# Second dense block: who copies out of PSUM, when the memory branch is gated, and in which order TensorE takes its products

## The reference

```python
h = rms_norm_2(x, g_mix);  proj = h @ w_in
u_ssm, q, k, v, qi, ki, wi, qm, gates = jnp.split(proj, offs, axis=-1)
y_ssm = s5_branch(u_ssm, ...)    # b_bar @ u, a complex linear scan over 256 tokens, real(c @ states),
                                 # + d_skip * u, gelu, then y * sigmoid(y @ w_glu)
y_dsa = dsa_branch(q, k, v, ...) # 8 heads of 64, keys chosen by an index score (a mask), softmax
y_mem = memory_branch(qm, km, vm)# 4 heads of 128 over 256 memory rows, softmax
g_s, g_d, g_m = jnp.split(jax.nn.sigmoid(gates), N_BRANCHES, axis=-1)
merged = g_s * (y_ssm @ w_up_ssm) + g_d * (y_dsa @ w_up_dsa) + g_m * (y_mem @ w_up_mem)
x = x + merged @ w_out
x = x + hier_moe(rms_norm_2(x, g_ffn), ...)   # 32 experts, all of w_gate, w_up, w_down read
```

## Time and profile before

| | us |
|---|---|
| median of 3 runs | 2243.97 |
| the profiled execution | 2246.94 |
| its span, first to last instruction | 2245.1 |
| TensorE busy | 1842.2 (82%) |
| VectorE busy | 812.1 (36%) |
| ScalarE busy | 497.7 (22%) |
| mean rate from memory over the span | 316 GB/s |

### The profile page before, as it was taken

One profiled execution on the slowest core, in us unless ns is written; L12 is line 12 of the kernel. 1 busy time (PEld: TensorE's weight loads), 2 busy tenths in 40 slices (PEclk: granted clock), 3 DMA queues, 4 the chain that ended last, 5 costly groups with the idle time before them and its releaser, 6 DMA issues. The chain is left out here.

```text
span 2245.1 us, 28438 instructions
## 1 busy us (share of the span) xinstructions
PE 1842.2 (82%) x11560; PEld 837.4 (37%) x11560; DVE 812.1 (36%) x1624; ACT 497.7 (22%) x1008; POOL 77.1 (3%) x96
## 2 busy tenths in 40 slices
PE   7899999899999989789987897698888845666555
PEld 3655545433433333234333232254534512222221
DVE  2224333333442344334443333587682300000001
ACT  2022311223232133332333333321301200000000
POOL 0000000000000000000000000093000000000000
PEclk9999999899999999889999999799999878787777
DMA  7744349498898799999999999443128299999996
GB/s 273 279 152 167 131 161 351 159 425 355 328 421 365 283 424 423 423 423 396 423 422 424 422 424 422 148 145 120 41 94 339 98 429 427 427 428 427 427 428 259
DMA packets 113958, 713.56 MB, mean 318 GB/s; under 512 B 16703, under 2 KB 21007, under 8 KB 68655
## 3 DMA queue, kind: packets, MB, share of 16 engines
q1 hardware_dynamic: 105344, 704.98, 77.1%
q10 hardware_dynamic: 8398, 5.47, 0.8%
HBM read 709.35 MB, written 1.07 MB: 316 GB/s over the span
## 5 line engine op out<-in xcount | busy, mean ns | idle before, releaser
L841 PE MATMUL ps<-ring,ar 128*32 128x512 f32 x3072 | 377.1, 631 | 62.4 <-DMA ring<-in_w 42.9
L459 PE MATMUL ps<-ar 128*128 128x128 f32 (+5 forms) x1742 | 352.9, 359 | 29.1 <-PEq L737 5.7
L466 PE MATMUL ps<-ring,ar 128*32 128x512 f32 x1184 | 208.7, 713 | 157.9 <-DMA ring<-in_w_gate 79.6
L459 PEld LDWEIGHTS ps<-ar 128*128 128x128 f32 (+2 forms) x1742 | 233.4, 200 | 154.0 <-issue 105.2
L459 PE MATMUL ps<-ring,ar 128*128 128x512 f32 (+2 forms) x592 | 248.4, 579 | 5.1 <-ACT ar L2201 2.6
L841 PEld LDWEIGHTS ps<-ring,ar 128*32 128x32 f32 x3072 | 97.2, 113 | 334.9 <-issue 264.1
L1738 DVE TENSOR_SCALAR ar<-ps 128x256 f32<-128x256 f32 x128 | 54.3, 425 | 438.3 <-PE ps L841 429.0
L853 PE MATMUL ps<-ring,ar 128*32 128x512 f32 x1536 | 175.1, 602 | 0.0
L574 PE MATMUL ps<-ring,ar 128*128 128x512 f32 x384 | 171.7, 597 | 0.0
L459 PEld LDWEIGHTS ps<-ring,ar 128*128 128x128 f32 x592 | 112.8, 192 | 134.3 <-issue 127.7
L2322 ACT ACTIVATE ar<-ps 64x512 f32<-64x512 f32 x256 | 151.5, 592 | 46.6 <-PE ps L853 32.5
(11 more groups left out here) (396 smaller groups left out, 1377.5 us busy)
## 6 DMA issues: line engine op xcount, KB each, us to landing
ring<-in_w SPq DMA_DIRECT2D x192, 2048.0 KB, 20.9
ring<-in_w_gate SPq DMA_DIRECT2D x26, 2048.0 KB, 26.0
ring<-in_w_up SPq DMA_DIRECT2D x24, 2048.0 KB, 26.2
ring<-in_w_down SPq DMA_DIRECT2D x24, 2048.0 KB, 24.0
ring<-in_w_in SPq DMA_DIRECT2D x21, 2048.0 KB, 8.1
ring<-in_w_ada SPq DMA_DIRECT2D x12, 2048.0 KB, 8.1
ar<-in_w_up SPq DMA_DIRECT2D x8, 2048.0 KB, 25.7
ar<-in_w_down SPq DMA_DIRECT2D x8, 2048.0 KB, 28.8
```

Of the source, the lines that this page charges most:

```text
L459: ins = self.t.e.matmul(o, l, r, start=(i == 0), stop=(i == len(pairs) - 1))
L466: ins = self.t.e.matmul(b[32 * i:32 * i + 32, :], l, r, start=(k == 0), stop=(k == len(steps) - 1))
L841: ins = e.matmul(b[32 * s:32 * s + 32, :], HG[:, 2 * c + r, 32 * n:32 * n + 32], W[:, r, HALF(s)], start=False, stop=(c == 3 and r == 1))
```

## The change

ScalarE takes over three sets of copies out of PSUM that VectorE made: the turned memory queries, the four scan weight matrices, and the values of all twelve attention units. The preparation copies stand after four gate evictions instead of five. In the loop the copy of unit k-3 stands behind the exponentials of unit k. The loop keeps three gate halves instead of five, and the other ten follow it. The memory branch is gated after the third scan instead of before it. TensorE takes `up(2, 0)` before `states(3)` and `up(2, 1)` behind it, then `glu`, then `up(1, ...)` and `up(0, ...)`. Slots, lanes and the order of the transfers follow.

```diff
@@ sync @@
-        up(2, 0, (1,))
         q.wait_ge(s_pe, pe["pv", 2, 11])
         up(2, 1, (7,))
+        up(2, 0, (0,))
+        fetch(("glu",), kpn(a["w_glu_2"][0]), 4, 512, lane=(1,))
         up(1, 0, (2,))
         up(1, 1, (0,))
-        fetch(("glu",), kpn(a["w_glu_2"][0]), 4, 512, lane=(1,))
-        up(0, 0, (7,))
-        up(0, 1, (2,))
-        lanes = (3, 4, 5, 6, 8, 7, 2, 0, 1)
+        lanes = (3, 4, 5, 6, 7, 8, 1, 2, 0)
         q.wait_ge(s_pe, pe["sy", 3])
         for k, (nm, u, i) in enumerate(units):
             if k == 3:
-                out2(0, (0,))
-                out2(1, (1,))
+                up(0, 0, (7,))
+                up(0, 1, (1,))
                 q.wait_ge(s_dve, dve["branch", 2, 0])
             if k == 4:
+                out2(0, (2,))
+                out2(1, (0,))
+            if k == 5:
                 q.wait_ge(s_pe, pe["up", 0, 1, 1])
@@ tensor_dense2 @@
-        t.wait_ge(s_dve, dve["lbc"])
-        t.wait_ge(s_act, act["u"])
+        t.wait_ge(s_act, act["lc", 1])
         driven(0)
...
-            if s < 5:
+            if s < 3:
                 gate_half(t, w, 2, 11 + s)
...
+        mids = (2, 3, 4, 5)
         driven(1)
         states(0)
-        (gates 16, 17)
+        gates(14, 15)
         driven(2)
-        (gates 18 to 21)
+        gates(16, 17, 18)
         states(1)
         driven(3)
-        (gates 22, 23)
-        t.wait_ge(s_dve, dve["branch", 2, 2])
-        up(2, 0, side)
-        up(2, 1, side)
+        gates(19, 20, 21, 22, 23)
         states(2)
-        t.wait_ge(s_dve, dve["branch", 2, 1])
-        up(1, 0, side)
+        t.wait_ge(s_act, act["branch", 2, 2])
+        up(2, 0, mids)
         states(3)
-        up(1, 1, side)
+        up(2, 1, mids)
         t.wait_ge(s_act, act["yg"])
         (glu, four products)
+        t.wait_ge(s_act, act["branch", 2, 1])
+        up(1, 0, mids)
+        up(1, 1, mids)
         t.wait_ge(s_dve, dve["branch", 2, 0])
-        up(0, 0, ALL)
-        up(0, 1, ALL)
+        up(0, 0, (7, 0, 1, 6))
+        up(0, 1, (7, 0, 1, 6))
@@ vector_dense2 @@
         index(1)
-        dve["qmT"] = turned_v(v, "qmT", QMT, 4, vcol("g_qm"))
-        (copies of lb 0, lc 0, lb 1, lc 1)
...
-            if s >= 2:
-                (wait for pv of unit s - 2, copy it to OM or OD2)
             scan_step(0, s)
...
         skip(1)
-        gated(2, 0)
-        gated(2, 1)
         scans(3)
         skip(2)
         skip(3)
         dve["tc"] = v.n
+        gated(2, 0)
+        gated(2, 1)
+        v.wait_ge(s_act, act["glu"])
+        dve["branch", 2, 0] = v(v.own.tensor_tensor(OSS, YG, SGT, ALU.mult))
         gated(1, 0)
         gated(1, 1)
@@ scalar_dense2 @@
-        for g in range(5):
+        for g in range(4):
             scalar_gate(s, 2, g)
+        (copies of qmT 0 to 3, lb 0, lc 0, lb 1, lc 1)
+        scalar_gate(s, 2, 4)
+
+        def values(u):
+            s.wait_ge(s_pe, pe["pv", 2, u])
+            (copy to OM or OD2)
+            read["pv", 2, u] = s.mark()
         for k in range(14):
             if k >= 2:
                 scalar_turned_p(s, 2, k - 2, 4)
             if k < 12:
                 scalar_exps(s, 2, k, 256, 128.0 ** -0.5 if k < 4 else 0.125, False)
-            if k < 5 and k % 2 == 0:
+            if k >= 3:
+                values(k - 3)
+            if k in (1, 3):
                 scalar_gate(s, 2, 5 + k // 2)
-        for g in range(8, 12):
+        values(11)
+        for g in range(7, 12):
             scalar_gate(s, 2, g)
```

More of the change, by code:

```diff
@@ L996, in tensor_dense2 @@
         gate_half(t, w, 2, 10)
-        t.wait_ge(s_dve, dve["qmT"])
-        t.wait_ge(s_act, act["qk2"])
         def scores(u):
@@ L1056, in up, with gates @@
             w.free("up", n, h)
-        side = (0, 1, 6)
+        def gates(*halves):
+            for i in halves:
+                gate_half(t, w, 2, i)
+        mids = (2, 3, 4, 5)
         driven(1)
         states(0)
-        for i in (16, 17):
-            gate_half(t, w, 2, i)
+        gates(14, 15)
         driven(2)
-        for i in (18, 19, 20, 21):
-            gate_half(t, w, 2, i)
+        gates(16, 17, 18)
         states(1)
         driven(3)
-        for i in (22, 23):
-            gate_half(t, w, 2, i)
-        t.wait_ge(s_dve, dve["branch", 2, 2])
-        up(2, 0, side)
-        up(2, 1, side)
+        gates(19, 20, 21, 22, 23)
         states(2)
-        t.wait_ge(s_dve, dve["branch", 2, 1])
-        up(1, 0, side)
+        t.wait_ge(s_act, act["branch", 2, 2])
+        up(2, 0, mids)
         states(3)
-        up(1, 1, side)
+        up(2, 1, mids)
         t.wait_ge(s_act, act["yg"])
@@ L1081, in tensor_dense2 @@
         for f in range(4):
-            b = w.claim("glu", f)
+            b = w.claim("glu", f, lane=(0, 1, 6))
             pe["glu", f] = w.sums(b[:, 0:256], [(W[:, k, TB(f)], YG[:, k, :]) for k in range(4)])
         w.free("glu")
+        t.wait_ge(s_act, act["branch", 2, 1])
+        up(1, 0, mids)
+        up(1, 1, mids)
         t.wait_ge(s_dve, dve["branch", 2, 0])
-        up(0, 0, ALL)
-        up(0, 1, ALL)
+        up(0, 0, (7, 0, 1, 6))
+        up(0, 1, (7, 0, 1, 6))
         tensor_out(t, w, 2)
@@ L2001, in vector_dense2 @@
             v(v.own.tensor_tensor(GATE[2 + h], GATE[2 + h], GATE[4 + h], ALU.add))
-        v.wait_ge(s_act, act["glu"])
-        dve["branch", 2, 0] = v(v.own.tensor_tensor(OSS, YG, SGT, ALU.mult))
         for h in range(2):
@@ L2421, in scalar_dense2 @@
         root(s, nrm[:, 0:8], "qm")
-        for g in range(5):
+        for g in range(4):
             scalar_gate(s, 2, g)
+        for c in range(4):
+            s.wait_ge(s_pe, pe["qmT", c])
+            s(s.own.activation(QMT[:, c, :], ps("qmT", c)[:, 0:256], ACT.Copy, scale=vcol("g_qm")))
+            read["qmT", c] = s.mark()
+        four = lambda name, i: ps(name, i)[:, :].rearrange("p (c q) -> p c q", c=4)
+        for i in range(2):
+            s.wait_ge(s_pe, pe["lb", i])
+            s(s.own.activation(LB[i], four("lb", i), ACT.Copy))
+            read["lb", i] = s.mark()
+            s.wait_ge(s_pe, pe["lc", i])
+            act["lc", i] = s(s.own.activation(LC[i], four("lc", i), ACT.Copy, scale=(1.0, -1.0)[i]))
+            read["lc", i] = s.mark()
+        scalar_gate(s, 2, 4)
+        def values(u):
+            s.wait_ge(s_pe, pe["pv", 2, u])
+            b = ps("pv", 2, u)
+            if u < 4:
+                k = s(s.own.activation(OM[:, 2 * (u % 2):2 * (u % 2) + 2, TB(u // 2)],
+                                       b[:, 0:256].rearrange("p (i q) -> p i q", i=2), ACT.Copy))
+            else:
+                k = s(s.own.activation(OD2[:, u % 4, TB((u - 4) // 4)], b[:, 0:128], ACT.Copy))
+            read["pv", 2, u] = s.mark()
+            if u == 3:
+                act["branch", 2, 2] = k
+            if u == 11:
+                act["branch", 2, 1] = k
         for k in range(14):
```

## The result

The changed kernel takes 2260.74 us (median of 4 runs, 2260.46 to 2264.76), the kernel before 2243.62 (4 runs). The ratio is 1.0081, with an interval of 1.0058 to 1.0105: slower by 17 us, more than the 11.2 us that the prediction counted as no change. The time lies in the range given; that it would be no change had been the likeliest case. The profiled execution took 2261.02 us with a span of 2259.2 and a mean clock of 0.915 (before 2246.94, 2245.1 and 0.919).

What follows compares the result with a forecast made beforehand. Memory paces the last stage, so the dense block's end sets the total; terms summed to -1.0 us at full clock, plus 9 for the clock: 2252 on the median's footing; own range 2245 to 2260, 8-in-10 range 2234 to 2268.

Steps and rivals of the forecast that it cites:

- What bounds the kernel: Experts' weights from memory pace the last stage, so the end is the dense block's end plus a constant.
- Preparation, -9.1: Before the loop: ScalarE's copies remove TensorE's wait for the second scan weight, so the loop begins 9.1 us earlier.
- The serial loop: Attention loop from step 3: values waits for ScalarE's copy out of bank 7; steps of 5.18 us against 3.57.
- the first rival: The loop keeps its pace: ScalarE's copy hides in idle time, 15.5 us less, total 2227.5; chance 0.10.
- The clock, +9: In the loop, TensorE's pauses lower its clock in nearly four slow steps, adding 9 us.
- The turn-in of quarter 1, -1.7: After the loop: VectorE starts this turn-in at about 1617.8, when driven(1) delivers, 1.7 us earlier.
- The memory gates, -8.65, and their cover: Gating behind the last scan takes 8.65 us off VectorE's chain; TensorE's late gate halves keep four microseconds of cover.
- The products, +9.4: Behind states(3): six product groups instead of four, putting 9.4 us back on.
- The loop keeps its pace: Rival: ScalarE's copy is hidden in its idle time and no slow clock, total 2227.5; chance 0.10.
- Serial at full clock: Rival: the loop is serial but the clock stays full, total 2243; chance 0.22.
- The loop stays at 1.2 GHz: Rival: pauses in bank 7's ring keep the clock low until the gate halves behind the loop, 2268; chance 0.20.
- unit 9 within 10 us of 1791.7: Sign: the experts' weight unit 9 is issued within some 10 us of its earlier time, 1791.7.

Runs made afterwards that it cites:

- a1_prep: The kernel before with only the eight preparation copies (turned queries, scan weight matrices) moved to ScalarE behind the fourth gate eviction; 2236.86 us, ratio 0.9964.
- b3_fill: The changed kernel with five spare 128x256 matmuls into unused bank 1 in TensorE's pause of loop steps 3 to 11; 2246.28 us, ratio 1.0003.
- a2_values: The kernel before with only the loop's attention value copies moved to ScalarE, behind the exponentials; five gate halves kept in the loop; 2263.34 us, ratio 1.0087.
- b1_bank: The changed kernel with two banks, 7 and 1, in turn for the attention values; 2230.66 us, ratio 0.9941.
- a3_tail: The kernel before with only the memory gates behind the last scan and the new order of products, queue and slots; 2245.81 us, ratio 1.0002.
- b2_order: The changed kernel with ScalarE's copy of unit k-3 ahead of the exponentials of unit k instead of behind them; 2236.38 us, ratio 0.9955.
- c0_slots: b1_bank with other slots: up(2, 0) and up(1, 1) in slot 1, glu and up(0, 1) in slot 0; 2234.01 us, ratio 0.9955.

## Why the prediction was right in its parts and short in its size

- **What bounds the kernel.** Right. From the experts' first product to the end of the span it was 460.4 to 462.3 us in all ten profiled executions, so the dense block's end sets the end. The new order of slots and transfers cost nothing there, as forecast.
- **Preparation, -9.1.** Right: 9.06 us, by the same steps. ScalarE's copies ran from 1533.47 to 1538.40; counted from the gate halves, `driven(0)` stands at 33.6 us, as forecast. a1_prep shows it alone (ratio 0.9964, 7.5 us by the medians).
- **The serial loop.** Right in mechanism and in price. The forecast was a step of 5.18 us and a loop of 66.1; b3_fill, at full clock, has 5.04 and 65.22, and the one step of a2_values at full clock 5.03. Against a loop without the wait that is 13.7 us where 15.5 was worked out for the first rival.
- **The clock, +9.** This is the term that failed, by its size: 17.0 us by the stages, 14.5 by the medians. I took nearly four slow steps out of eleven at 2.4 us each. In fact all steps from the fifth on were slow: eight by 1.4 to 2.0 us against b3_fill, and the last two by 0.7 and 0.9. The clock came back at the end of a step's work or in the pause, and was at 0.50 again for the next scores. "The clock may also come back" was true and saved little. The two rows that I set against each other were of stretches with a few pauses. They could not decide on a loop in which every round has one.
- **The turn-in of quarter 1, -1.7.** Wrong, and only in part by the clock. VectorE did wait for `driven(1)` (4.94 us), but that group ran at half speed (2.11 us) and the turn-in began 2.11 us behind its start, against 1.76 before. At full clock (b1_bank, b3_fill) it began 1.17 us behind, where 0.4 was forecast.
- **The memory gates, -8.65, and their cover.** The move is right: quarter 3's turn-in follows `skip(1)` at once, as the rows of VectorE after show beside the earlier trace rows.

```profile
1628.48 0.69 DVE L1907 TENSOR_TENSOR ar<-ps,ring 128x512 f32<-128x512 f32 x1 [4.94 <-PE ps L460]
...
1667.97 0.48 DVE L1949 SCALAR_TENSOR_TENSOR ring<-ring,ar,ps 128x256 f32<-128x256 f32 x1
1668.56 0.69 DVE L1907 TENSOR_TENSOR ar<-ps,ring 128x512 f32<-128x512 f32 x1
...
1688.00 0.48 DVE L1949 SCALAR_TENSOR_TENSOR ring<-ring,ar,ps 128x256 f32<-128x256 f32 x1
```

  The four microseconds of cover were mis-sized. `skip(2)` ended at 1688.48 and `states(3)` began at 1690.46, so TensorE was last, by some 2 us: `up(2, 0)` waited 3.45 us for a weight whose slot came free at 1676.4, and then ran 8.83 us instead of 7.03. The five gate halves that free this slot began 30.0 us behind `driven(1)` and took 20.0; the forecast had 26.7 and 17.2. Even where the loop ran at full clock (b1_bank) they began 28.3 us behind it and took 19.1. There and in a3_tail and b3_fill the stage is 61.5 to 61.9 us, where 60.3 was forecast.

```profile
1676.41 0.37 SPq L312 DMA_DIRECT2D ring<-in_w_up_mem  x1
```

  That row is the queue's, in the timeline after: the megabyte was issued when the slot came free, and the product began 5.3 us later.
- **The products, +9.4.** Right: 9.1 us in the changed kernel and the same in a3_tail. Together the two moves of the tail are worth nothing, as forecast (-1.0) and as measured (a3_tail, ratio 1.0002).
- **The rivals.** "The loop keeps its pace" is the kernel that b1_bank and b2_order make (2230.66 and 2236.38 us; forecast 2227.5), not the one that was changed. "Serial at full clock" is b3_fill (2246.28; forecast 2243). "The loop stays at 1.2 GHz" (2268) lies 7.3 us above the result, the forecast of 2252 lies 8.7 below it; what happened lies between: slow in every step, but for two thirds of it. The Trainium skill (TensorE: Matmul & The Clock Gate, Loop structure matters more than you think) shows a loop with a long wait for a DMA in every round, whose matmuls run cold. The waits here are for ScalarE and take 2.25 us; the trace agrees for the scores of each step but not for the whole step, and the 25 us worked out for eleven slow steps are above the 17.0 measured.

The sum by its terms, in us: -9.1 + 22.3 (13.7 + 14.4 of it on top of a loop that is 5.8 shorter without the wait) - 6.3 + 9.1 + 1.4 = +17.4. The forecast's sum was +8.0. Of the 9.4 us between them the clock has 8.0, the scans' stage at full clock 1.2 (61.47 against 60.3) and the stage behind `tensor_out`'s first transposes 1.4, which the change was not expected to touch (59.9 to 62.0 us over all ten kernels); the loop at full clock and the products give 1.2 back. So the total fell inside the range given although the clock's term was half of what was measured. Of the signs named, unit 9 within 10 us of 1791.7 did not come true: it was issued at 1804.53, 17.4 us later when counted from the gate halves.

## What to carry to other kernels

When a copy out of PSUM moves to another engine, look at what stands ahead of it in that engine's stream, and whether that work depends on the product which waits for the bank: here this closed a ring through three engines. A wait of 2 us that comes back in each round of a TensorE loop must be priced twice, once as time and once as clock, and here the clock was about half of the loss. Before tuning such a loop, fill the pause with spare products once: it separates the two prices in one run.

## What was not expected of the hardware

The clock's swing in the changed kernel: with pauses of 2.25 to 2.36 us between some 4 us of work, the scores of the steps from the fifth on ran wholly or for the most part at 1.2 GHz, and 1.00 was granted mainly in the pauses and at the edges of the work (the first product behind the pause took 0.66 us, as at full clock, at 1606.39, 1613.05 and 1619.73). The same kernel gets 14.5 us faster by doing 45 matmuls (90 records) more. That such pauses always do this is not shown: a2_values kept 1.00 over one whole step with the same pause. What decides it stays open.

Single waits of about 2 us are no guide. After a wait of 2.04 us the transposes of `tensor_out` took 2.93 us in the changed kernel and 1.97 in a2_values, a3_tail and c0_slots; the products behind a wait of 2.28 took 20.87 us in a3_tail and 22.56 in c0_slots. But for the slots, the changed kernel and c0_slots run the same code there. What tells these cases apart stays open.
